# Two weight chunks ahead of x in the load queue and in the order of ScalarE and VectorE

## The chip, the cores and the metric

The kernel runs on one core of one Trainium2 chip. The metric is the device time of one execution in microseconds, as the median of several runs. Times inside the execution come from one profiled execution and count from the start of its span.

## The reference

One layer of a streaming encoder is computed in float32 for 512 prompt tokens and 32 sample tokens, T = 544 tokens of width 1024:

```python
r = x + 0.5 * rms_norm(swiglu_ffn(rms_norm(x, norm_ffn1_pre), w_ffn1_gate_up, w_ffn1_down), norm_ffn1_post)
z = rms_norm(r, norm_mix_pre) @ w_in          # then window attention and a gated short convolution
r = r + rms_norm(mixed @ w_out, norm_mix_post)
r = r + 0.5 * rms_norm(swiglu_ffn(rms_norm(r, norm_ffn2_pre), w_ffn2_gate_up, w_ffn2_down), norm_ffn2_post)
gate = sigmoid(rms_norm(r, norm_ple_pre) @ w_ple_gate)
r = r + rms_norm(gate * (p @ w_ple_proj), norm_ple_post)
```

The two feed-forward layers have an inner width of 2816, so the gate and up matrix is 1024 x 5632. Only the very beginning matters here: x, its norm, and the first columns of w_ffn1_gate_up.

## The kernel before

Features lie on partitions and tokens on the free axis. The 544 tokens are two halves A and B of 272. The residual r, and x_hi and x_lo made of it, have 8 feature tiles each (KD = 8).

Every float32 product is made of three matmuls in a rounded format: the weight is rounded to w_hi on ScalarE (`split_hi`, line 474), and the rest w_lo = raw - w_hi is made on VectorE (`split_lo`, line 796). The same holds for x: x_hi is r times a gain, rounded, on ScalarE (line 489), and x_lo is the rest, on VectorE (line 826). The products are w_hi x_hi, w_lo x_hi and w_hi x_lo.

Weights come in chunks of 128 columns, 512 KB each in the up stages (rows of 512 bytes), into four slots `raw`, `w_hi`, `w_lo`. The load of chunk c waits for w_lo of chunk c - 4. All large loads are issued by SyncE into one queue in program order: four tiles of x_prompt (512 KB each, rows of 4 KB), x_sample (128 KB), weight chunks 0 to 3, then some small gain rows and the copies of cache rows (`load_gains`), then the other weight chunks in loops.

Each engine has an order of its own, written out by hand; semaphores join them. At the start:

- TensorE turns x with transposes (line 1326): for each feature tile k four of 128 tokens into PSUM, then the sample's. The first four wait for the four x tiles one by one. Then comes the first pass of up1 on half A (`hi_pass`, line 1247): w_hi and w_lo times x_hi for chunks 0 and 1 over all k, then for chunks 2 and 3. Each chunk's first matmul waits for its w_lo (`up_ready`). In the pass of chunks 2 and 3, ahead of k = 2, stands the sum of the squares over partitions (`all_sums(0)`, line 1234). Then `lo_pass` (line 1255) adds w_hi times x_lo for the four chunks. Half B follows in the same form; its first matmul waits until VectorE has scaled half A's first gate result out of PSUM (line 834). From there on loops of full products (lines 1217 to 1219) run.
- VectorE copies the even feature tiles of r out of PSUM (line 943) and ScalarE the odd ones (line 597). VectorE squares half A's tiles (`first_square`, line 936) into two alternating buffers `sq`; GpSimd adds each to `ssq` (lines 418, 421). Square k waits for addition k - 2.
- ScalarE makes x_hi of half A in pairs, and rounds chunks 0 and 1 between them (`if k in (4, 6)`), then chunks 2 and 3. Then it goes on with half B: x_hi and squares, with the root of the first sum after the third tile.
- VectorE does square 4, w_lo 0, squares 5 and 6, w_lo 1, square 7, w_lo 2, x_lo of A tiles 0 to 3, w_lo 3, x_lo of A tiles 4 to 7, then the reciprocal of the root (line 802), x_lo of B, and the scaling of the first results.

Of the kernel before, what the change touches and what calls it, by code (L numbers as in the profile page):

```python
# [17 lines left out]
def encoder_layer(nc, t):  # L18
# [16 lines left out]
    KD = D // P  # L35
# [22 lines left out]
    chunks = units = 0  # L58
    for name, n, un, kt in STAGES:
        C0[name], U0[name] = chunks, units  # L60
        chunks, units = chunks + n, units + un
# [7 lines left out]
    def loaded_value(c):  # L69

        return 16 * sum(loads_of[c % SLOTS:c + 1:SLOTS])
# [33 lines left out]
    with ctx:  # L105
# [164 lines left out]
        def half(tile, k, h):  # L270
            return tile[:, k, h * HT:(h + 1) * HT]
# [36 lines left out]

        @block.sync
        def _(sp):  # L310
            def load_up(s, i):
                for j in range(4):
                    c = C0[s] + j
                    if isinstance(i, int):
                        if c + 4 * i >= SLOTS:
                            sp.wait_ge(lo_made, c + 4 * i - SLOTS + 1)
                    else:
                        sp.wait_ge(lo_made, i * 4 + (c - SLOTS + 1))
                    sp.dma_start(raw[:, c % SLOTS, 0:KD, :], up[s][j % 2, i * 2 + j // 2])\
                        .then_inc(w_loaded[c % SLOTS], 16)  # L320

            def load_down(s, i):
                for j in range(4):
                    c = C0[s] + j
                    sp.wait_ge(lo_made, i * 4 + (c - SLOTS + 1))
                    sp.dma_start(raw[:, c % SLOTS], down[s][i * 2 + j // 2, j % 2])\
                        .then_inc(w_loaded[c % SLOTS], 16)

            def load_short(cs):
                for c in cs:  # L330
                    sp.wait_ge(lo_made, c - SLOTS + 1)
                    for dst, src in chunk_loads(c):
                        sp.dma_start(dst, src).then_inc(w_loaded[c % SLOTS], 16)

            def load_gains():
                rows = "a (k p) -> (a k) p"
                for name in ("norm_ffn1_post", "norm_mix_pre", "norm_mix_post", "norm_ffn2_pre", "norm_ffn2_post",
                             "norm_ple_pre", "norm_ple_post"):
                    sp.dma_start(g_rows[COL[name]:COL[name] + KD, :], t[name].rearrange(rows, p=P)).then_inc(g_in, 16)
                for name, n, src in (("norm_conv_out", KA, t["norm_conv_out"].rearrange(rows, p=P)),  # L340
                                     ("conv_w", 3 * KA, t["conv_w"].rearrange("a j (k p) -> (a j k) p", p=P)),
                                     ("cache_conv", 2 * KA, t["cache_conv"].rearrange("a b j (k p) -> (a b j k) p", p=P))):
                    sp.dma_start(g_rows[COL[name]:COL[name] + n, :], src).then_inc(g_in, 16)
                at = COL["norm_attn_out"]
                for e in range(2):
                    sp.dma_start(g_rows[at:at + KA, e * DH:(e + 1) * DH],
                                 t["norm_attn_out"][0, e * DA // 2:(e + 1) * DA // 2].rearrange("(k p) -> k p", p=DH))\
                        .then_inc(g_in, 16)

                for name in "kv":  # L350
                    sp.dma_start(t[f"new_{name}_sample"][0, 0, 0:WINDOW - DEC], t[f"cache_attn_{name}"][0, 0, DEC:WINDOW])\
                        .then_inc(state_moved, 16)

            for i in range(XT - 1):
                sp.dma_start(x_tok[:, i, :], t["x_prompt"][0, i * P:(i + 1) * P, :]).then_inc(x_in[i], 16)
            sp.dma_start(x_tok[0:DEC, XT - 1, :], t["x_sample"][0]).then_inc(x_in[XT - 1], 16)
            for s, d in (("up1", "down1"), ("up2", "down2")):
                load_up(s, 0)
                if s == "up1":
                    load_gains()  # L360
                with sp.Fori(1, UP_GROUPS) as i:
                    load_up(s, i)
                with sp.Fori(0, DOWN_GROUPS) as i:
                    load_down(d, i)
                if s == "up1":
                    mix, flat, rows = C0["mix"], "a b w g d -> (a b w) (g d)", "a b j (k p) -> (a b j k) p"
                    load_short(range(mix, mix + SLOTS))

                    sp.wait_ge(unit_done, U0["mix"])
                    for name, dst in (("k", k_cache), ("v", v_cache)):  # L370
                        sp.dma_start(dst[:], t[f"cache_attn_{name}"][0, 0].rearrange("w g d -> w (g d)")).then_inc(cache_in, 16)
                    sp.dma_start(sinks[:], t["attn_sinks"].to_broadcast([P, 8])).then_inc(sink_in, 16)
                    load_short(range(mix + SLOTS, mix + 4 * SLOTS))
                    sp.wait_ge(band_ready, 3)
                    for name, prompt, sample in (("k", k_new[:], k_own[:]), ("v", v_band[:, NCH - 2, :], v_own[:])):
                        sp.dma_start(t[f"new_{name}_prompt"].rearrange(flat), prompt).then_inc(state_stored, 16)
                        sp.dma_start(t[f"new_{name}_sample"].rearrange(flat)[WINDOW - DEC:WINDOW, :], sample)\
                            .then_inc(state_stored, 16)
                    load_short(range(mix + 4 * SLOTS, C0["up2"]))
                    sp.wait_ge(conv_out, 1)  # L380
                    for name, at in (("prompt", 0), ("sample", 2 * KA)):
                        sp.dma_start(t[f"new_conv_{name}"].rearrange(rows, p=P), conv_new[at:at + 2 * KA, :])\
                            .then_inc(state_stored, 16)
# [82 lines left out]
        def _(act):  # L466
            def split_hi(c, i=0):

                n, s = width_of[c], c % SLOTS
                act.wait_ge(w_loaded[s], i * 16 + loaded_value(c))  # L470
                if c >= SLOTS:
                    semaphore, value, per = used(c - SLOTS)
                    act.wait_ge(semaphore, i * per + value)
                nc.scalar.activation(w_hi[:, s, 0:n, :], raw[:, s, 0:n, :], ACT.Copy).then_inc(hi_made, 1)  # L474
# [115 lines left out]
            act.dma_start(g_rows[0:KD, :], t["norm_ffn1_pre"].rearrange("a (k p) -> (a k) p", p=P)).then_inc(g_first_in, 16)  # L590
            act.wait_ge(consts, 4)
            nc.scalar.activation(rms_first[:], eps[:], ACT.Sqrt)
            act.wait_ge(g_made, 1)
            for k in range(KD):
                if k % 2:
                    act.wait_ge(x_turned, k + 1)
                    nc.scalar.activation(r[:, k, 0:SEQ], misc[:, k % 4, :], ACT.Copy).then_inc(r_loaded_act, 1)
                    act.wait_ge(r_loaded, k // 2 + 1)
                    high(0, k - 1, A)
                    act.wait_ge(r_loaded_act, k // 2 + 1)  # L600
                    high(0, k, A)
                if k in (4, 6):
                    split_hi(k // 2 - 2)
            split_hi(2), split_hi(3)
            act.wait_ge(r_loaded, KD // 2 + 1)
            up_stage("up1", 0, KD, 1)
# [184 lines left out]
        def _(dve):  # L791
            def split_lo(c, i=0):

                n, s = width_of[c], c % SLOTS
                dve.wait_ge(hi_made, i * 4 + (c + 1))
                nc.vector.tensor_tensor(w_lo[:, s, 0:n, :], raw[:, s, 0:n, :], w_hi[:, s, 0:n, :].bitcast(F32),  # L796
                                        ALU.subtract).then_inc(lo_made, 1)
# [133 lines left out]
            def first_square(k):  # L931

                if k >= 2:
                    dve.wait_ge(summed, k - 1)
                dve.wait_ge(r_loaded_act if k % 2 else r_loaded, k // 2 + 1)
                nc.vector.tensor_tensor(sq[:, k % 2, :], half(r, k, A), half(r, k, A), ALU.mult)\
                    .then_inc(first_squared, 1)

            dve.wait_ge(turned_g, 1)
            nc.vector.tensor_copy(gT[:, 0:KD], bank[:, 0, 0:KD]).then_inc(g_made, 1)  # L940
            for k in range(0, KD, 2):
                dve.wait_ge(x_turned, k + 1)
                nc.vector.tensor_copy(r[:, k, 0:SEQ], misc[:, k % 4, :]).then_inc(r_loaded, 1)
                first_square(k // 2)
            dve.wait_ge(x_turned, KD + 1)
            nc.vector.tensor_copy(r[:, :, SEQ:T], bank[:, 3, 0:KD * DEC].rearrange("p (k n) -> p k n", k=KD))\
                .then_inc(r_loaded, 1)
            first_square(4)
            split_lo(0)
            first_square(5), first_square(6)  # L950
            split_lo(1)
            first_square(7)
            split_lo(2)
            chain_lo(0, A, range(0, 4))
            split_lo(3)
# [149 lines left out]
            for v in range(2, len(MIX_UNITS)):  # L1105
# [12 lines left out]
                if v == 32:  # L1118
                    for s, at in enumerate((SEQ, T + 2)):
                        i = nc.vector.tensor_copy(conv_rows[:, s], cinp[:, :, at:at + 2].rearrange("p k r -> p r k"))  # L1120
# [487 lines left out]
```

## Time and profile before

| | |
|---|---|
| median of 3 runs | 1155.08 us (1153.62 to 1156.03) |
| span of the profiled execution | 1152.4 us |
| TensorE busy | 1107.6 us (96%) |
| VectorE busy | 570.2 us (49%) |
| ScalarE busy | 422.3 us (37%) |
| GpSimd busy | 133.5 us (12%) |
| moved by DMA | 94.28 MB, mean 82 GB/s |

The span goes from the first to the last instruction on the engines; what lies around it in a timed run is not part of it. The busy shares are means over the whole span. The change touches its first 40 us, so the stretches of that part must be read by themselves.

### The profile page before, as it was taken

To read this page: it belongs to the slowest core of one execution; us is meant where nothing else is said; L and a number is where in the kernel's file an instruction comes from. 1 tells how busy PE (TensorE), PEld (TensorE's weight loads), DVE (VectorE), ACT (ScalarE), POOL (GpSimd) and SP (SyncE) were. 2 spreads that over 40 slices of the span, in tenths; PEclk is the share of its full clock that TensorE was granted. 3 is DMA by queue.
4 is the path that set the end of the run, shared out by engine and by line. 5 is a ranking of instruction groups with operands and counts; after the bars stand their busy time and mean duration, and the time that the engine had idled before them with its cause. 6 is when DMAs were issued, how large, how long until landed. Compare 5 with 4: busy or idle time off the path is not lost.

```text
span 1152.4 us, 21208 instructions
## 1 busy us (share of the span) xinstructions
PE 1107.6 (96%) x8503; PEld 1076.5 (93%) x8503; DVE 570.2 (49%) x1029; ACT 422.3 (37%) x803; POOL 133.5 (12%) x154
## 2 busy tenths in 40 slices
PE   5999999999999999999989889999999999998896
PEld 5999999999999999877888889999999999998896
DVE  6644445444312268556593784445444421226743
ACT  4533333223222254423444562333323322225563
POOL 3100000000011132000213420000000001113211
PEclk8999999999999999999999999999999999999899
DMA  7232333223333205121032222233322333333002
GB/s 212 73 91 73 89 93 105 77 73 102 99 101 100 74 20 121 32 60 55 20 110 74 74 67 80 73 91 94 106 73 73 110 95 98 101 92 88 24 1 78
DMA packets 182644, 94.28 MB, mean 82 GB/s; under 512 B 11768, under 2 KB 180928, under 8 KB 182592
## 3 DMA queue, kind: packets, MB, share of 16 engines
q1 hardware_dynamic: 182576, 93.56, 28.4%
q8 instruction: 36, 0.59, 0.2%
q14 instruction: 16, 0.13, 0.0%
q10 hardware_dynamic: 16, 0.00, 0.0%
HBM read 91.15 MB, written 2.50 MB: 81 GB/s over the span
## 4 chain that ended last, share of the span: by engine, by line
PE 85%; DVE 10%; ACT 2%; POOL 1%; issue 1%; DMA 1%; SPq 0%; DVEq 0%; POOLq 0%; ACTq 0%
PE bank L1219 25%; PE bank L1217 25%; PE bank L1218 25%; PE bank L1247 3%; DVE x_lo L826 2%; PE misc L1326 2%; PE misc L1389 2%; DVE w_lo L796 2%; PE misc L1368 1%; POOL ssq L421 1%; DVE r L817 1%; ACT w_hi L474 1%; PE bank L1255 1%; DVE rpre L802 1%; DVE misc L802 1%
## 5 line engine op out<-in xcount | busy, mean ns | idle before, releaser
L1217 PE MATMUL bank<-x_hi,w_hi 128*128 128x272 f32 x1600 | 464.9, 291 | 5.2 <-DVE tG L1154 3.3
L1219 PE MATMUL bank<-x_hi,w_lo 128*128 128x272 f32 x1600 | 464.6, 290 | 0.0
L1218 PE MATMUL bank<-x_lo,w_hi 128*128 128x272 f32 x1600 | 461.2, 288 | 0.0
L796 DVE TENSOR_TENSOR w_lo<-raw,w_hi 128x1024 fp32r<-128x1024 f32 (+2 forms) x154 | 206.6, 1348 | 275.9 <-ACT w_hi L474 275.9
L1217 PEld LDWEIGHTS bank<-x_hi,w_hi 128*128 128x128 f32 x1600 | 302.3, 189 | 9.6 <-issue 6.7
L1218 PEld LDWEIGHTS bank<-x_lo,w_hi 128*128 128x128 f32 x1600 | 302.9, 189 | 0.1
L1219 PEld LDWEIGHTS bank<-x_hi,w_lo 128*128 128x128 f32 x1600 | 302.0, 189 | 0.0
L474 ACT ACTIVATE w_hi<-raw 128x1024 fp32r<-128x1024 f32 (+2 forms) x154 | 173.7, 1135 | 177.4 <-PE bank L1219 161.6
L1219 PE MATMUL bank<-h_hi,w_lo 128*128 128x272 f32 x704 | 204.5, 290 | 0.0
L1217 PE MATMUL bank<-h_hi,w_hi 128*128 128x272 f32 x704 | 204.2, 290 | 0.0
L1218 PE MATMUL bank<-h_lo,w_hi 128*128 128x272 f32 x704 | 203.0, 288 | 0.0
L421 POOL TENSOR_TENSOR ssq<-ssq,sq 128x272 f32<-128x272 f32 x112 | 108.0, 964 | 253.0 <-ACT sq L479 242.2
L1218 PEld LDWEIGHTS bank<-h_lo,w_hi 128*128 128x128 f32 x704 | 133.3, 189 | 0.2
L1217 PEld LDWEIGHTS bank<-h_hi,w_hi 128*128 128x128 f32 x704 | 133.0, 189 | 0.2
L1219 PEld LDWEIGHTS bank<-h_hi,w_lo 128*128 128x128 f32 x704 | 133.0, 189 | 0.0
L505 ACT ACTIVATE tG<-tG 128x272 f32<-128x272 f32 x88 | 38.0, 431 | 132.7 <-DVE tG L834 132.7
L418 POOL COPY ssq<-sq 128x272 f32<-128x272 f32 x16 | 10.9, 683 | 620.2 <-ACT sq L479 611.3
L511 ACT ACTIVATE h_hi<-tU 128x272 f32 (+1 forms) x88 | 38.0, 431 | 122.0 <-DVE tU L843 122.0
L1247 PE MATMUL bank<-x_hi,w_hi 128*128 128x272 f32 x224 | 64.3, 317 | 11.1 <-DVE w_lo L796 3.8
L836 DVE TENSOR_TENSOR tU<-bank,rpre 128x272 f32<-128x272 f32 x88 | 38.4, 436 | 66.7 <-PE bank L1219 66.7
L845 DVE TENSOR_TENSOR h_lo<-tU,h_hi 128x272 f32 (+1 forms) x88 | 39.3, 447 | 62.2 <-ACT h_hi L511 62.2
L479 ACT ACTIVATE sq<-bank 128x272 f32<-128x272 f32 x48 | 18.9, 393 | 118.8 <-PE bank L1219 116.1
(160 smaller groups left out, 1073.0 us busy)
## 6 DMA issues: line engine op xcount, KB each, us to landing
raw<-w_ffn_gate_up SPq DMA_DIRECT2D x88, 512.0 KB, 3.9
raw<-w_ffn_down SPq DMA_DIRECT2D x32, 704.0 KB, 4.7
raw<-w_in SPq DMA_DIRECT2D x14, 512.0 KB, 3.9
raw<-w_ple_gate SPq DMA_DIRECT2D x8, 512.0 KB, 3.9
x_tok<-x_prompt SPq DMA_DIRECT2D x4, 512.0 KB, 5.0
raw<-w_in SPq DMA_DIRECT2D x8, 256.0 KB, 4.2
raw<-w_out SPq DMA_DIRECT2D x16, 128.0 KB, 2.9
raw<-w_out SPq DMA_DIRECT2D x8, 256.0 KB, 3.4
```

What stands on the lines that cost most here:

```text
L421: nc.gpsimd.tensor_tensor(dst, dst, sq[:, s % 2, :], ALU.add).then_inc(summed, 1)
L474: nc.scalar.activation(w_hi[:, s, 0:n, :], raw[:, s, 0:n, :], ACT.Copy).then_inc(hi_made, 1)
L505: nc.scalar.activation(tG[:, j, :], tG[:, j, :], ACT.Silu).then_inc(gate_act, 1)
L511: nc.scalar.activation(half(h_hi, i * 2 + j, h), tU[:, j, :], ACT.Copy).then_inc(h_hi_made, 1)
L796: nc.vector.tensor_tensor(w_lo[:, s, 0:n, :], raw[:, s, 0:n, :], w_hi[:, s, 0:n, :].bitcast(F32), ALU.subtract).then_inc(lo_made, 1)
L802: nc.vector.reciprocal(dst, sum_bank(n)).then_inc(inverted, 1)
L836: nc.vector.tensor_tensor(tU[:, j, :], psum(u + 1), rpre[:, h, :], ALU.mult).then_inc(u_scaled, 1)
L845: nc.vector.tensor_tensor(half(h_lo, i * 2 + j, h), tU[:, j, :], half(h_hi, i * 2 + j, h).bitcast(F32), ALU.subtract).then_inc(h_ready[h], 1)
L1217: nc.tensor.matmul(psum(u), wh, hi, start=(k == 0), stop=False)
L1218: nc.tensor.matmul(psum(u), wh, lo, start=False, stop=False)
L1219: mm = nc.tensor.matmul(psum(u), wl, hi, start=False, stop=(k == n - 1))
L1247: nc.tensor.matmul(psum(u), w[:, c % SLOTS, k, :], half(x_hi, k, h), start=(k == 0 and w is w_hi), stop=False)
```

## The change

The loads of chunks 0 and 1 are issued ahead of x, those of chunks 2 and 3 stay behind it. ScalarE rounds chunks 0 and 1 ahead of its first work on x (before it waits for the first gains), and VectorE makes their w_lo right behind its copy of the first gains, ahead of its first copy of x. Squares 4 to 7 then stand together.

```diff
-            def load_up(s, i):
-                for j in range(4):
+            def load_up(s, i, chunks=range(4)):
+                for j in chunks:
...
+            load_up("up1", 0, range(2))
             for i in range(XT - 1):
                 sp.dma_start(x_tok[:, i, :], t["x_prompt"][0, i * P:(i + 1) * P, :]).then_inc(x_in[i], 16)
...
-                load_up(s, 0)
+                load_up(s, 0, range(2 if s == "up1" else 0, 4))
...
             nc.scalar.activation(rms_first[:], eps[:], ACT.Sqrt)
+            split_hi(0), split_hi(1)
             act.wait_ge(g_made, 1)
...
-                if k in (4, 6):
-                    split_hi(k // 2 - 2)
             split_hi(2), split_hi(3)
...
             nc.vector.tensor_copy(gT[:, 0:KD], bank[:, 0, 0:KD]).then_inc(g_made, 1)
+            split_lo(0), split_lo(1)
             for k in range(0, KD, 2):
...
-            first_square(4)
-            split_lo(0)
-            first_square(5), first_square(6)
-            split_lo(1)
-            first_square(7)
+            for k in range(KD // 2, KD):
+                first_square(k)
             split_lo(2)
```

## Rows read from the trace of the kernel before

**Rows 1.** The page: span, busiest engine, and the chain by engine.
```profile
span 1152.4 us, 21208 instructions
...
PE 1107.6 (96%) x8503; PEld 1076.5 (93%) x8503; DVE 570.2 (49%) x1029; ACT 422.3 (37%) x803; POOL 133.5 (12%) x154
...
PE 85%; DVE 10%; ACT 2%; POOL 1%; issue 1%; DMA 1%; SPq 0%; DVEq 0%; POOLq 0%; ACTq 0%
```

**Rows 2.** Stretches: length, busy per engine, granted clock, DMA share, GB/s.
```profile
3.00:8.00 5.00, 1.67 (x4) 0.73 (x4) 0.17 (x1) 0.00 (x0) 0.00 (x0) 1.00 1.00 388
9.00:15.00 6.00, 6.00 (x32) 5.83 (x31) 3.77 (x7) 4.54 (x9) 1.94 (x3) 1.00 1.19 288
15.40:17.80 2.40, 0.10 (x2) 0.00 (x0) 2.34 (x5) 2.40 (x6) 1.86 (x2) 1.00 0.20 46
17.90:20.70 2.80, 0.75 (x2) 0.43 (x2) 2.80 (x4) 2.21 (x3) 2.28 (x3) 0.50 0.57 162
20.80:24.50 3.70, 3.70 (x16) 3.70 (x17) 3.70 (x5) 1.91 (x5) 3.18 (x4) 0.50 0.63 174
24.60:26.60 2.00, 2.00 (x17) 1.95 (x16) 2.00 (x3) 0.00 (x1) 1.09 (x2) 0.99 0.81 237
...
35.80:37.00 1.20, 0.00 (x0) 0.00 (x0) 1.20 (x4) 0.04 (x1) 0.00 (x0) 1.00 0.00 0
...
50.00:1145.00 1095.00, 1070.53 (x8261) 1041.80 (x8261) 534.17 (x976) 396.67 (x757) 118.03 (x130) 0.99 0.28 79
```

**Rows 3.** The chain that ended last, in its first 80 us: start, us, what.
```profile
26.13 1.15 DVE w_lo L796
...
31.23 5.35 DVE x_lo L826 x8
...
37.08 6.27 PE bank L1247 x48
```

**Rows 4.** Timeline of TensorE: start, us, operation, idle before it and releaser.
```profile
8.81 6.08 PE L1326 MATMUL misc<-ident,x_tok 128*128 128x128 f32 x29 [1.19 <-DMA x_tok<-x_prompt]
...
17.86 0.57 PE L1247 MATMUL bank<-x_hi,w_hi 128*128 128x272 f32 x1 [2.35 <-ACT x_hi L489]
...
20.78 0.59 PE L1247 MATMUL bank<-x_hi,w_hi 128*128 128x272 f32 x1 [2.13 <-DVE w_lo L796]
...
27.32 0.39 PE L1247 MATMUL bank<-x_hi,w_hi 128*128 128x272 f32 x1 [0.55 <-DVE w_lo L796]
...
28.18 0.62 PE L1234 MATMUL misc<-ssq,ones 128*128 128x272 f32 x2
```

**Rows 5.** Timeline of VectorE around the squares of x.
```profile
16.54 1.21 DVE L796 TENSOR_TENSOR w_lo<-raw,w_hi 128x1024 fp32r<-128x1024 f32 x1
...
18.60 0.43 DVE L936 TENSOR_TENSOR sq<-r 128x272 f32<-128x272 f32 x1
18.95 1.78 DVE L796 TENSOR_TENSOR w_lo<-raw,w_hi 128x1024 fp32r<-128x1024 f32 x1
20.65 0.99 DVE L936 TENSOR_TENSOR sq<-r 128x272 f32<-128x272 f32 x1
21.57 1.21 DVE L796 TENSOR_TENSOR w_lo<-raw,w_hi 128x1024 fp32r<-128x1024 f32 x1
```

**Rows 6.** Timeline of GpSimd: additions of the squares.
```profile
13.85 0.77 POOL L421 TENSOR_TENSOR ssq<-ssq,sq 128x272 f32<-128x272 f32 x1 [0.94 <-DVE sq L936]
...
21.72 1.69 POOL L421 TENSOR_TENSOR ssq<-ssq,sq 128x272 f32<-128x272 f32 x1 [0.38 <-DVE sq L936]
```

**Rows 7.** SyncE's queue: four chunks issued; the page's line with us to landing.
```profile
3.48 7.56 SPq L319 DMA_DIRECT2D raw<-w_ffn_gate_up  x4
...
raw<-w_ffn_gate_up SPq DMA_DIRECT2D x88, 512.0 KB, 3.9
```

**Rows 8.** Timeline of ScalarE: rounding of chunks 2 and 3.
```profile
17.70 2.00 ACT L474 ACTIVATE w_hi<-raw 128x1024 fp32r<-128x1024 f32 x2
```

**Rows 9.** Transposes by tile: ns min/median/max, first and last start.
```profile
L1326 PE MATMUL misc<-ident,x_tok x32: 272/421/477, 4.6 to 14.6; 128*128 128x128 f32 x32
...
L1326 PE MATMUL misc<-ident,y_gain x32: 270/273/327, 1128.6 to 1144.6; 128*128 128x128 f32 x32
```

## The prediction

> **What bounds the kernel now.** I read the page first. TensorE is busy 96% of a 1152.4 us span and carries 85% of the chain that ended last; VectorE has 10% of it [rows 1]. Between 50 and 1145 us TensorE is busy 1070.5 of 1095 us [rows 2]. Nothing of the change touches that stretch: after the first four weight chunks every load, rounding and split stands in the same order behind the same waits. What the change can move is the moment from which TensorE runs through, and whatever moves that moment moves the end by the same amount.
>
> So I read the chain in order of time through the head of the kernel. It goes from x to the last of the four w_lo (26.13 to 27.3), to the first sum over squares on TensorE (28.18), and through the root on ScalarE and the reciprocal on VectorE to eight x_lo on VectorE (31.23 to 36.58). Then come the first scaled gate and the eight-chain of token half B on TensorE at 37.08 [rows 3, 4]. TensorE stands still from 35.8 to 37.0 [rows 2], so VectorE sets 37.08. I look at its timeline, since its order of work is what the change rewrites.
>
> VectorE has nothing to do until x comes: the last x tile is first turned at 8.81 [rows 4], and from 15.4 to 17.8 it is busy 2.34 of 2.40 us, from 17.9 to 24.5 all of it [rows 2]. Two of its operations there, the w_lo of chunks 0 and 1, start at 16.54 and 18.95 [rows 5] and do not depend on x. The change takes them out of this stretch and pays with a later x. The question is which of the two is larger.
>
> **Part 1, the load queue: x comes later.** The queue moves in order, so all of x moves behind two chunks of 524,288 bytes. In 9 to 15 us, when the queue holds only weight chunks, it moves 288 GB/s; in 3 to 8 us, when it holds x, it moves 388 GB/s [rows 2]. The two chunks take 2 x 0.524 MB / 288 GB/s = 3.64 us. The start of the queue on an empty chip with weights in front is not shown, so I bound it: if weights went at x's rate it would be 2 x 0.524 / 388 = 2.70 us; if the change from one kind to the other costs some 0.3 us on top, 3.9. I take 3.6, the rate of the very same transfers, so the last x tile is turned first at 12.4 instead of 8.81. The issue of the loads costs nothing beyond that: the four chunks took 7.56 us to issue [rows 7] only because the queue was full, and with two chunks and x in it x is at least as near to moving as the queue's head. Chunks 2 and 3 land when they did, since the bytes ahead of them are the same, and by 15.4 the queue is all but empty (46 GB/s) [rows 2]; their first use moves from 17.7 [rows 8] to about 20. The gains behind them are not needed for tens of us.
>
> The Trainium skill, DMA: Bandwidth & Descriptors, section Specifications, puts the smallest transfer that runs at line rate at 512 B. By that rule the weights' 512-byte rows would cost no more than x's 4 KB rows, and the delay would be 2.7 instead of 3.6 us. The measured 288 against 388 GB/s speaks against it.
>
> **Part 2, ScalarE: two roundings leave.** The roundings of chunks 0 and 1 ran between the copies of x and x_hi. They now run at about 4.7 and 6.6 us (a chunk lands 3.9 us after its issue [rows 7], here at 0.7, and the second 1.8 later), where ScalarE waits for x anyway. Here and below I use the clock of before and add the 3.6 at the end. x_hi 6 and 7 end at 16.5 instead of 17.7, and chunk 2's and 3's roundings (2.00 us from 17.70 [rows 8]) end at 18.5. The four w_lo of chunk 2 and 3 need them only later, so by itself this brings nothing on the path.
>
> **Part 3, VectorE: two splits leave.** w_lo 0 runs from 16.54 to the next start at 17.68 (1.14 us) and w_lo 1 from 18.95 to 20.65 (1.70 us) [rows 5]: 2.84 us less behind x. They now run at about 6 to 9 us, in cover: VectorE waits for the first copy of x, then at about 13 us, so 4 us of slack stand behind them. But all 2.84 is not won. The squares of x alternate with GpSimd's additions: square k waits for addition k-2, and the two buffers are shared. In before the w_lo filled those waits. An addition takes 0.77 alone, and 1.69 when it starts beside a w_lo (21.72), ending 0.63 after that w_lo [rows 5, 6]; a square starts 0.35 before the next operation (18.60, 18.95) [rows 5]. Without filler, from 16.54, which is where square 4 ends: square 5 0.36, addition 4 0.63, its semaphore 0.15, addition 5 ahead of square 6 0.63, squares 6 and 7 0.72, addition 6 ahead of w_lo 2 0.63. Together 3.12, so w_lo 2 starts at 19.7 instead of 21.57: the gain is 1.9 us. Its bounds are 1.6 (each addition 0.77) and 2.84 (no stall). From there to w_lo 3 the order is unchanged.
>
> Sum so far: w_lo 3 comes 3.6 - 1.9 = 1.7 us later, and so does all that hangs on it.
>
> **Part 4, TensorE: a new pause ahead of the critical sum.** In before the first pass of chunks 0 and 1 starts at 17.86, stops for w_lo 1 until 20.78 and hands over to chunks 2 and 3 at about 26.6, so that only 0.55 us are lost before 27.32 [rows 3, 4]. After the change the pass follows the turning of x directly. In before's clock it runs from 15.4 to about 19.4 (32 matmuls at 0.12), and then TensorE waits: two matmuls when w_lo 2 is there (20.8), the rest when w_lo 3 is (25.3). Two gaps of 1.4 and 4.3 us stand where one of 0.55 was. In before, the granted clock is 0.50 (1.2 GHz) from 17.9 to 24.5, behind a pause of 2.4 us with 0.10 us of work in it, and back at 1.00 (2.4 GHz) after 3.7 us of work [rows 2]. There the slow stretch cost nothing, because TensorE was ahead of w_lo 3. Now it would lie behind it. At half clock 16 matmuls took 3.70 us, at full clock 17 took 2.00 [rows 2], that is 0.23 against 0.12 each. Six of them and the sum over squares, which showed 0.62 at full clock, stand between w_lo 3 and the root: 6 x 0.11 = 0.6, plus 0.3 to 0.5 for the sum. I take 0.9 us. TensorE's own path then: 64 matmuls at 0.12 and the sum's 0.6 from 29.0 on, 16 of the matmuls slow: 29.0 + 8.3 + 1.8 = 39.1. That is just ahead of VectorE's 37.08 + 1.7 + 0.9 = 39.7, so VectorE still decides.
>
> The sum is +1.7 + 0.9 = +2.6 us. The profiled execution has a span of 1152.4, and the median of the runs is 1155.1, 2.7 us more, which I take as what lies around the span. Only the difference is carried over: 1155.1 + 2.6 = 1157.7.
>
> **The rivals.**
> - *The clock stays up, or is up sooner.* If the two matmuls at w_lo 2 or the place of the pause keep the clock at 1.00, part 4 is nothing: +1.7, 1156.8. The turning of x may gain too: the median transpose there took 421 ns where the last ones of the kernel take 273 [rows 9], though the clock is printed as 1.00, so for most of them the engine was slow; if it quickens sooner after the later x, up to 1 us comes back, 1155.8. For it: the head of the trace shows one fall only, and there is work on both sides of the new pause. Against it: that one fall came after 2.4 us, and the pause here has 4.3.
> - *Stalls smaller and loads quicker.* Weights at 2.7 us, gain 2.84: -0.1, and with the clock +0.8: 1155.0 to 1155.9. For it: the two bounds. Against it: each is the far end.
> - *Faster.* The loads overlap so well that x is not later than by about 1 us; then the gain of 1.9 wins, and with the clock or without it is -0.9 to -2.8, 1152.3 to 1154.2. It decides the sign from the point at which x's delay is below the gain. Against it: both rates are steady for microseconds, and DMA is busy all through 3 to 15 us.
> - *The clock stays down longer.* If 26 of the 64 matmuls are slow, TensorE's own path ends at 29.0 + 8.3 + 2.9 = 40.2, and with the sum later too +3.5: 1158.6.
>
> **How the numbers follow.** Forecast 0.45 (own range 1157.1 to 1158.4), clock up 0.25, stalls smaller 0.13, faster 0.08, clock down longer 0.09. 0.2% is 2.3 us, about what a measurement of this kernel can tell from no change. The forecast lies just outside it, at +2.6; 0.04 of its 0.45 falls inside. So faster 0.08, same 0.25 + 0.13 + 0.04 = 0.42, slower 0.50. The range leaves out the faster case and the lower half of the smaller stalls (0.14) and a tail above (0.05): 1155.4 to 1159.0.
>
> **What would show it.** The first turning of the last x tile at 12.4 (part 1). w_lo 0 and 1 over by 9 us (part 3). Squares 5 to 7 with idle VectorE between them, and w_lo 2 starting at about 23.3. The first pass of chunks 0 and 1 from about 19 without a stop, then a pause and w_lo 3 ending near 29. The granted clock at 0.50 in the slices behind that. Half B's first matmul at 39.7, and all later stages as before. The prediction is wrong if x is late by less than 2.7 us or more than 3.9, if VectorE is not the last before half B, or if the later stages differ.

## The result

| | before | changed |
|---|---|---|
| median, seven runs each | 1153.64 us (1152.91 to 1156.03) | 1157.26 us (1156.19 to 1159.14) |
| span of the profiled execution | 1152.4 us | 1155.5 us |
| ratio to before | | 1.0024, 95% interval 1.0013 to 1.0035 |

The change makes the kernel slower, by 0.24%, which is 2.8 us, and the whole interval lies above 1 (1.5 to 4.0 us). The two medians alone lie 3.6 us apart, inside that interval. Beside the experiments the kernel before had medians of 1154.83 to 1155.04 over 23 to 29 runs, so 1153.64 is a low one. The forecast was +2.6 us.

Nothing large shows on the page of the changed kernel. Line numbers have moved by up to two (1247 is 1245, 1217 is 1215).

```profile
span 1155.5 us, 21208 instructions
...
PE 1107.5 (96%) x8503; PEld 1075.6 (93%) x8503; DVE 569.5 (49%) x1029; ACT 422.6 (37%) x803; POOL 132.0 (11%) x154
...
PE 83%; DVE 10%; ACT 3%; POOL 2%; issue 1%; DMA 1%; SPq 0%; DVEq 0%; POOLq 0%; ACTq 0%
```

Busy times are those of before to within 1.5 us per engine, as they must be: the same instructions run. The chain carries two per cent less TensorE and one more each of ScalarE and GpSimd. Two per cent are about 20 us, and TensorE's whole part of the chain in the first 40 us of before is under 8, so the chain also takes other ways through the later joints between stages, and its shares say little on the change.

The stretches of the changed kernel answer to [rows 2]; the columns are length, busy per engine, granted clock, DMA share and GB/s.

```profile
3.00:7.00 4.00, 0.00 (x0) 0.00 (x0) 1.10 (x1) 1.47 (x2) 0.00 (x0) 1.00 1.12 328
7.00:11.00 4.00, 0.95 (x2) 0.36 (x2) 1.35 (x2) 0.64 (x1) 0.00 (x0) 1.00 1.02 410
...
24.50:28.50 4.00, 0.16 (x2) 0.00 (x0) 4.00 (x6) 1.16 (x3) 2.31 (x4) 0.70 0.46 131
26.60:28.50 1.90, 0.00 (x0) 0.00 (x0) 1.90 (x3) 0.00 (x0) 0.50 (x1) 0.50 0.43 130
28.60:32.80 4.20, 4.20 (x16) 3.97 (x17) 2.63 (x5) 1.54 (x5) 0.24 (x1) 0.50 0.47 128
33.00:35.00 2.00, 2.00 (x18) 2.00 (x17) 1.97 (x3) 2.00 (x6) 1.71 (x3) 1.00 0.00 0
```

The first two rows show the new order of the queue: weights at 328 GB/s (by 7 us some 1.5 MB have moved and the two chunks are 1.05, so the end of this stretch is x already; the single stretches 3 to 4 and 4 to 5 us have 329 and 328), then x at 410. From 24.5 to 28.5 TensorE has almost nothing to do, which is the new pause. The granted clock falls to 0.50 in it, near 26.1, and stays there through the first 4.2 us of work behind it.

The timeline of TensorE, which answers to [rows 4], shows the same as single operations.

```profile
12.99 4.77 PE L1324 MATMUL misc<-ident,x_tok 128*128 128x128 f32 x29 [1.44 <-DMA x_tok<-x_prompt]
...
18.30 0.39 PE L1245 MATMUL bank<-x_hi,w_hi 128*128 128x272 f32 x1
...
24.15 0.39 PE L1245 MATMUL bank<-x_hi,w_hi 128*128 128x272 f32 x1 [1.55 <-DVE w_lo L796]
...
28.59 0.59 PE L1245 MATMUL bank<-x_hi,w_hi 128*128 128x272 f32 x1 [3.93 <-DVE w_lo L796]
...
39.50 0.36 PE L1245 MATMUL bank<-x_hi,w_hi 128*128 128x272 f32 x1 [0.43 <-DVE tG L834]
```

The last x tile is turned 4.18 us later than before, and the turning of the other tiles is quicker (4.77 against 6.08 us). The first pass follows without a wait, and then come the two pauses for w_lo 2 and w_lo 3. Half B starts at 39.50 instead of 37.08.

So the way from x to half B can be cut into four pieces. The start of the sample tile's transposes marks the end of the turning.

| piece | before | changed | difference |
|---|---|---|---|
| first turning of the last x tile, at | 8.81 | 12.99 | +4.18 |
| from there to the end of the turning | 6.01 | 4.70 | -1.31 |
| to the end of w_lo 3 | 12.44 | 10.85 | -1.59 |
| to the root on ScalarE | 1.58 | 2.72 | +1.14 |
| to half B's first matmul | 8.24 | 8.24 | 0.00 |
| half B starts at | 37.08 | 39.50 | +2.42 |

The spans differ by 3.1 us. The 0.7 us that half B does not carry come from later stages, which are looked at under the prediction.

### The profile page after: what moved, and what is told of

The parts are those of the page before. It is cut to its first block, busy times and chain, and to the rows that moved or that the text cites. A ratio compares the mean times of both kernels' runs of the same rounds, so it can differ in the third digit from the quotient of the medians.

```text
span 1155.5 us, 21208 instructions
## 1 busy us (share of the span) xinstructions
PE 1107.5 (96%) x8503; PEld 1075.6 (93%) x8503; DVE 569.5 (49%) x1029; ACT 422.6 (37%) x803; POOL 132.0 (11%) x154
## 4 chain that ended last, share of the span: by engine, by line
PE 83%; DVE 10%; ACT 3%; POOL 2%; issue 1%; DMA 1%; SPq 0%; DVEq 0%; POOLq 0%; ACTq 0%
PE bank L1217 25%; PE bank L1215 25%; PE bank L1216 25%; DVE x_lo L826 2%; PE bank L1245 2%; PE misc L1324 2%; PE misc L1387 2%; DVE w_lo L796 2%; POOL ssq L422 1%; PE misc L1366 1%; DVE r L817 1%; DVE rpre L802 1%; DMA x_tok<-x_prompt 1%; DVE misc L802 1%; ACT w_hi L475 1%
```

## The experiments

Each experiment was timed in five rounds beside the kernel before on the same chip. The ratios carry intervals of 0.09% to 0.17% on each side, which is 1 to 2 us, so they can tell only the larger differences. The smaller ones are read from the traces, where half B's start follows a chain of single operations. There is one trace of each kernel, and the head scatters too: in the four kernels with both chunks ahead of x in the queue and x turned by the same operations, the last x tile came between 12.93 and 13.39 and the turning took 4.70 to 5.45 us. "Half B" is its first matmul, and "turning" is the time from the first transpose of the last x tile to the first one of the sample tile.

| kernel | last x tile | turning | w_lo 3 ends | to the root | half B | ratio to before |
|---|---|---|---|---|---|---|
| before | 8.81 | 6.01 | 27.26 | 1.58 | 37.08 | 1 |
| changed | 12.99 | 4.70 | 28.54 | 2.72 | 39.50 | 1.0024 (1.0013 to 1.0035) |
| loads alone | 13.22 | 5.13 | 31.11 | 1.72 | 41.05 | 1.0043 (1.0026 to 1.0060) |
| order of engines alone | 8.69 | 10.74 | 30.02 | 1.57 | 39.93 | 1.0037 (1.0022 to 1.0053) |
| changed, pauses filled | 13.39 | 5.09 | 29.36 | 1.56 | 39.16 | 1.0015 (1.0002 to 1.0027) |
| changed, w_lo 2 earlier | 12.93 | 5.45 | 28.84 | 2.73 | 39.80 | 1.0023 (1.0013 to 1.0034) |
| before, warm | 8.61 | 4.96 | 26.32 | 1.67 | 36.22 | 0.9993 (0.9980 to 1.0005) |
| one chunk ahead | 11.15 | 5.77 | 28.44 | 1.58 | 38.24 | 0.9998 (0.9987 to 1.0010) |
| changed, three repairs | 12.80 | 3.41 | 27.37 | 1.57 | 37.17 | 1.0000 (0.9990 to 1.0011) |
| before, warmer | 10.02 | 3.35 | 26.51 | 1.73 | 36.48 | 0.9998 (0.9989 to 1.0006) |
| before, warmer and filled | 9.58 | 3.35 | 26.12 | 1.58 | 35.94 | 1.0001 (0.9991 to 1.0011) |

### The loads alone

```diff
+            load_up("up1", 0, range(2))
             for i in range(XT - 1):
...
-                load_up(s, 0)
+                load_up(s, 0, range(2 if s == "up1" else 0, 4))
```

> The kernel before with the load order of the change alone: weight chunks 0 and 1 ahead of x, roundings and w_lo where they were. My theory (x late against work taken off VectorE): the last x tile is turned first at 13.0 us, as in the changed kernel. Behind it VectorE has the two w_lo again, so w_lo 3 ends at 30.1 to 30.7 us instead of 28.5, and half B starts at 40.3 us, or 41.4 if the clock is at half behind w_lo 3; the time is 1.0 to 2 us above the changed kernel, ratio to before 1.003 to 1.004. Rival (moving the roundings and w_lo is worth nothing, only the load order counts): half B at 39.5 as in the changed kernel, ratio 1.0024.

The last x tile came at 13.22, w_lo 3 ended at 31.11 and half B started at 41.05, for a ratio of 1.0043. That is 1.6 us later than the changed kernel at half B, and 2.57 us later at w_lo 3. VectorE has the two w_lo between its squares again:

```profile
20.38 1.21 DVE L797 TENSOR_TENSOR w_lo<-raw,w_hi 128x1024 fp32r<-128x1024 f32 x1
21.52 1.35 DVE L937 TENSOR_TENSOR sq<-r 128x272 f32<-128x272 f32 x2
22.80 1.78 DVE L797 TENSOR_TENSOR w_lo<-raw,w_hi 128x1024 fp32r<-128x1024 f32 x1
```

The rival, that moving the work is worth nothing, falls by the trace: from the end of the turning to the end of w_lo 3 it is 12.76 us, and 10.85 with the work moved. The intervals of the two times overlap. The late x alone is dear, and the moved work gives part of it back. It does not pay a slow clock behind w_lo 3 (1.72 us to the root), so the net gain of the moved work at half B is smaller than its gain at w_lo 3. The expectation of 40.3 was 0.7 us too early, because x came 0.2 us later, and the turning (0.43 us more than in the changed kernel) and the way to w_lo 3 were longer than assumed.

### The order of the engines alone

```diff
-            load_up("up1", 0, range(2))
...
-                load_up(s, 0, range(2 if s == "up1" else 0, 4))
+                load_up(s, 0)
```

> The changed kernel with the loads as they were: x first, then four chunks, but ScalarE and VectorE still take chunks 0 and 1 ahead of x. My theory: both engines stand in front of x until chunk 1 has landed (near 12.8 us), VectorE's first copy of x comes at about 15.1 instead of 9.3 us, w_lo 3 ends near 29.3, half B starts at 39.2, or 40.3 with the clock at half: ratio to before 1.002 to 1.003, so the new order of the engines needs the new order of the loads. Rival (the order of the engines costs nothing, the late x is all): ratio 1.000, half B at 37.1.

VectorE's first copy of x came at 15.08, as expected, behind w_lo 1. TensorE shows who was held up:

```profile
8.69 3.04 PE L1323 MATMUL misc<-ident,x_tok 128*128 128x128 f32 x13 [1.12 <-DMA x_tok<-x_prompt]
15.82 3.68 PE L1323 MATMUL misc<-ident,x_tok 128*128 128x128 f32 x16 [4.10 <-DVE r L943]
```

The first 16 transposes fill the four PSUM banks; the rest stand for 4.10 us until VectorE has emptied one. Half B started at 39.93, 0.7 us later than expected, ratio 1.0037. There was a pause of 3.24 us ahead of w_lo 3 here too, but the granted clock fell only at about 31.5, behind the sum over squares (30.93), so the root came 1.57 us behind w_lo 3. TensorE was then at half clock until about 34.9, went through to half B without a pause, and was its last path by some 0.1 us (8.34 from the root instead of 8.24). Neither half of the change stands alone, and the two together are less bad than either (1.0024), though the intervals overlap.

### The pauses filled

```diff
+FILL1, FILL2 = 12, 30
...
                 if units[2:4]:
+                    if ci == 0 and h == A:
+                        pe.wait_ge(r_loaded_act, KD // 2)
+                        fill(FILL1)
+                        (u2, c2, ready2), (u3, c3, ready3) = units[2:4]
+                        ready2()
+                        fill(FILL2)
                     hi_pass(units[2:4], x_hi, h, lambda k: None, second)
...
+            def fill(n):
+                for _ in range(n):
+                    nc.tensor.matmul(misc[:, 3, 0:HT], w_hi[:, 0, 0, :], half(x_hi, 0, A), start=True, stop=True)
```

> The changed kernel with matmuls that nobody needs (42 of 272 columns into a free PSUM bank) in TensorE's two pauses ahead of w_lo 2 and w_lo 3. If the clock at half behind the pause costs what I say, the granted clock stays at 1.00, the time from the end of w_lo 3 to the root falls from 2.7 to 1.6 us, and half B starts at 38.4 instead of 39.5: 1.1 us less than the changed kernel, ratio to before 1.0015. Rival (the clock is beside the path, or does not depend on the pause): half B at 39.5, ratio 1.0024 or more.

The granted clock stayed at 1.00 through the former pause. The first fence is the stretches of this kernel, the second its chain behind w_lo 3, and the third the chain of the changed kernel:

```profile
22.50:28.50 6.00, 5.95 (x48) 5.73 (x47) 5.77 (x7) 2.31 (x6) 4.85 (x6) 1.00 0.37 100
28.60:30.90 2.30, 2.14 (x16) 1.84 (x15) 2.30 (x5) 0.00 (x0) 0.00 (x0) 1.00 0.04 11
```

```profile
29.42 1.01 PE bank L1246 x6
30.43 0.47 PE misc L1233 x2
```

```profile
28.59 1.73 PE bank L1245 x6
30.32 0.92 PE misc L1232 x2
```

Six matmuls take 1.01 instead of 1.73 us, and the sum 0.47 instead of 0.92. From the end of w_lo 3 to the root it is 1.56 instead of 2.72. That 1.16 us is the price of the clock, and the empty pauses are its cause: nothing but work in the two pauses was added. Half B came only 0.34 us sooner, not 1.1, because in this execution x was 0.40 us later and the turning 0.39 us longer. The ratio of 1.0015 is the expected one, but its interval overlaps that of the changed kernel, so the gain is shown by the trace and not by the time.

### w_lo 2 between the squares

```diff
-            for k in range(KD // 2, KD):
-                first_square(k)
-            split_lo(2)
+            first_square(4), first_square(5), first_square(6)
+            split_lo(2)
+            first_square(7)
```

> The changed kernel with w_lo 2 between squares 6 and 7 instead of behind square 7. If VectorE's two idle pieces of 0.67 us between the squares are GpSimd's additions, one of them goes: w_lo 3 ends 0.4 to 0.7 us sooner (27.9 instead of 28.5), and half B starts near 38.9; ratio 0.0005 below the changed kernel. Rival (the additions of GpSimd then come later and the same time is lost at x_lo): no change.

In the changed kernel VectorE stands still twice between the squares, each time until an addition of GpSimd is over:

```profile
18.92 1.25 DVE L936 TENSOR_TENSOR sq<-r 128x272 f32<-128x272 f32 x2
20.84 0.44 DVE L936 TENSOR_TENSOR sq<-r 128x272 f32<-128x272 f32 x1 [0.67 <-POOL ssq L422]
21.95 0.44 DVE L936 TENSOR_TENSOR sq<-r 128x272 f32<-128x272 f32 x1 [0.67 <-POOL ssq L422]
22.31 1.78 DVE L796 TENSOR_TENSOR w_lo<-raw,w_hi 128x1024 fp32r<-128x1024 f32 x1
```

With w_lo 2 ahead of square 7 one of the two pieces went, and the end of w_lo 3 came 10.46 us behind the end of the turning instead of 10.85. That 0.39 is the lower end of what was expected. More had been won on the way: w_lo 3 started 8.69 us behind the end of the turning instead of 9.64. But it then took 1.77 instead of 1.21 us, as w_lo 2 does behind an addition of GpSimd, so 0.56 of the 0.95 us was lost again. That is in part the rival, that the additions come later and cost the same time elsewhere.

```profile
21.62 1.80 DVE L796 TENSOR_TENSOR w_lo<-raw,w_hi 128x1024 fp32r<-128x1024 f32 x1
27.07 1.77 DVE L796 TENSOR_TENSOR w_lo<-raw,w_hi 128x1024 fp32r<-128x1024 f32 x1
```

At half B nothing of it is seen, because the turning was 0.75 us longer in this execution. The clock stayed at half to about 34.4, so TensorE's own path came level with VectorE's. Its x_lo pass started at 35.73, and half B followed with no idle time before it:

```profile
35.73 4.11 PE L1253 MATMUL bank<-x_lo,w_hi 128*128 128x272 f32 x32
39.80 0.36 PE L1245 MATMUL bank<-x_hi,w_hi 128*128 128x272 f32 x1
```

It cost nothing all the same: from the root to half B it is 8.23 us, as in the changed kernel. The condition of the prediction's fourth rival, the clock down longer, was met, and its price was not paid. The ratio did not change.

### Before, with TensorE kept busy while x comes

```diff
+WARM, WARM_X = 10, 4
...
+            for _ in range(WARM):
+                turn(bank[:, 1, 0:P], ident[:])
             pe.wait_ge(g_first_in, 16)
...
                     if k == 0:
+                        if i:
+                            for _ in range(WARM_X):
+                                turn(bank[:, 1, 0:P], ident[:])
                         pe.wait_ge(x_in[i], 16)
```

> The kernel before with transposes that nobody needs ahead of and between the first tiles of x (10 from 1.7 us on, 4 behind each of the first tiles), into a free PSUM bank. If TensorE turns x at 1.2 GHz although the profile prints 1.00, the 29 transposes behind the last x tile fall from 6.0 us to 3.1 to 4, w_lo 3 ends 0.8 to 1.2 us sooner, half B starts at 36.0 to 36.3 instead of 37.1: ratio to before 0.999 to 0.9993. Rival (the turning is bound by the copies out of PSUM, or the clock was up): no change, 1.000.

The turning took 4.96 instead of 6.01 us, w_lo 3 ended 0.94 us sooner and half B started 0.86 us sooner, at 36.22; 0.20 of it is an earlier x. So about 1 us of the six was the clock, although the profile of before prints 1.00 through all of them. The turning did not come down to 4 us; the median transpose still took 391 ns. The trace shows why: the few transposes between the tiles did not keep the clock up. In this kernel the profile does record a fall, just as the last tile comes, and a rise near 12.1:

```profile
8.00:12.00 4.00, 3.39 (x16) 3.39 (x17) 2.17 (x4) 1.74 (x4) 0.46 (x2) 0.58 1.19 268
12.00:14.00 2.00, 2.00 (x22) 1.83 (x20) 1.63 (x4) 2.00 (x5) 1.23 (x2) 0.99 1.20 290
```

These rows have the columns of [rows 2]. The ratio of 0.9993 fits, with 1 inside its interval.

### One chunk ahead

```diff
-            load_up("up1", 0, range(2))
+            load_up("up1", 0, range(1))
...
-            split_hi(0), split_hi(1)
+            split_hi(0)
...
                     high(0, k, A)
+                if k == 4:
+                    split_hi(1)
...
-            split_lo(0), split_lo(1)
+            split_lo(0)
...
-            for k in range(KD // 2, KD):
-                first_square(k)
+            first_square(4), first_square(5), first_square(6)
+            split_lo(1)
+            first_square(7)
```

> Half of the change: chunk 0 alone ahead of x in the load queue, on ScalarE and on VectorE; chunk 1 is handled as before, with w_lo 1 between squares 6 and 7. The last x tile is turned first at 10.9 us (half the delay), w_lo 3 ends near 28.1, half B starts at 37.9, or 38.9 if the clock is at half behind w_lo 3: ratio to before 1.0007 to 1.0016, between the two kernels. Rival (a fixed cost of the new order, whatever the number of chunks): as the changed kernel, 1.0024.

The last x tile came at 11.15, 2.34 us after before and 1.84 ahead of the changed kernel. Half B started at 38.24, almost in the middle of the two. There is no fixed cost of the new order; each chunk ahead of x costs a share, but the two shares are made of different things. The first delayed x by 2.34 us and gained 0.92 between turning and w_lo 3, with no slow clock behind it. The second brought the slow clock (2.72 instead of 1.58 us to the root), and the quicker turning. The timed ratio of 0.9998 is below what was expected, and the upper end of its interval just takes in the 1.16 us of the trace.

### The changed kernel with three repairs

This is the filler of the pauses (6 and 32 matmuls), w_lo 2 between squares 6 and 7, and 36 useless transposes ahead of the first x tile and 5 ahead of each of the others.

> The changed kernel with three repairs at once: useless transposes ahead of x so that x is turned at full clock, useless matmuls in the two pauses so that the clock stays up, and w_lo 2 between squares 6 and 7. If the late x (4 us) is the only loss that is left and the three repairs give about 1, 1.1 and 0.4 us, half B starts at 37.0 to 37.5, as in the kernel before: ratio 1.000. Rival (the losses lie elsewhere): ratio above 1.0015.

x was as late as in the changed kernel, 12.80. The turning took 3.41 us, with a median transpose of 273 ns as at the end of the kernel [rows 9], and 1.57 us passed from w_lo 3 to the root:

```profile
L1336 PE MATMUL misc<-ident,x_tok x32: 272/273/329, 8.5 to 16.0; 128*128 128x128 f32 x32
```

Half B started at 37.17 and the ratio is 1.0000. The 4.0 us of late x are paid for by 2.60 us of quicker turning and 1.28 us less from its end to w_lo 3. The third repair cannot be seen by itself: that last way is 11.16 us long, more than the 10.85 of the changed kernel, and w_lo 3 took 1.79 us in it, as in the kernel with w_lo 2 earlier. So the account of the loss closes, in the trace and in the time.

### Warmer, and warmer and filled

Two attempts to better the kernel before: with 5, 8 and 12 useless transposes between the x tiles, and then also with transposes in the pauses ahead of w_lo 0, 1 and 3.

> The kernel before with more of the useless transposes between the first tiles of x (5, 8 and 12 instead of 4 each), so that the pauses of the turning are filled. Theory: the 29 transposes take 3.5 us (5.0 with fewer, 6.0 in before), w_lo 3 ends at 25.2 to 25.6, half B starts at 35.1 to 35.6: ratio to before 0.9983 to 0.9988. Rival (once VectorE's and ScalarE's copies bound the turning, no more is to be had): half B at 36.2 as with fewer.

> The same, with useless transposes also in the pauses ahead of w_lo 0, w_lo 1 and w_lo 3. Theory: the clock stays at 1.00 from the turning on, but in this order of loads the slow stretch lies ahead of w_lo 3 and costs nothing on the path, so half B starts within 0.4 us of the kernel without them: same ratio. Rival (the slow stretch now reaches past w_lo 3): up to 1.1 us less.

The transposes of the first ran at half clock for longer than I assumed and overran x: the last tile was turned first at 10.02 instead of 8.7. The turning took 3.35 us, about as expected (3.5), but half B started at 36.48, and not at 35.1 to 35.6; the rival had 36.2. The turning ended 0.20 us sooner than with fewer transposes, and w_lo 3 ended 0.19 us later, so a quicker turning was not passed on in full. What holds it up behind the turning was not tested.

Filling the pauses as well kept the granted clock at 1.00 throughout, and changed nothing behind w_lo 3 beyond 0.15 us (1.58 against 1.73 us to the root). That is the mechanism expected: with x first the slow stretch lies ahead of w_lo 3. Half B came 0.54 us sooner, outside the 0.4 that was stated, and 0.44 of it is that x was turned sooner. Half B is then 1.14 us ahead of before, but the time shows nothing of it (1.0001). Neither ratio differs from 1, so no kernel here is shown to be faster than the kernel before.

## Why the prediction was right, and where its terms were off

The sign and the size hold: +2.6 us forecast, +2.8 by the ratio, +2.4 at half B in the profiled execution. So do the three causes in the sum, late x, less work on VectorE and a slow clock behind the new pause. But two of the three signs of being wrong that the prediction names were met: x is late by more than 3.9 us, and the later stages differ. Only the third was not, since VectorE is the last before half B. The near hit is in part luck, as the terms show.

**Part 1, x later: 3.6 forecast, 4.18 measured.** This term was mis-sized, and beyond its upper bound of 3.9. The rate was not the reason: ahead of x the weights moved at 328 GB/s and not at 288 [rows 2], which alone gives 3.2. The step that failed is the sum itself, bytes divided by rate. The loads of one chunk and of two give the price that counts: the first x tile came at 4.58, 6.60 and 8.50 with none, one and two chunks ahead, so about 2.0 us per 512 KB. The last tile lost some 0.3 more, in both. In its first 3 us the queue had moved less than before (99 against 147 GB/s in 1 to 3 us), which is part of it. Where the rest lies, between the last byte and the landing, stays open. The rule of the Trainium skill (DMA: Bandwidth & Descriptors, section Specifications) that 512 B is enough for line rate would have given 2.7, an estimate with x's 388 GB/s; the runs speak against it, with 328 against 410 GB/s in one and the same kernel. No run varies the length of the rows alone.

**Parts 2 and 3, work taken from behind x: 1.9 forecast, 1.59 measured on VectorE.** w_lo 0 and 1 ran at 5.90 and 7.67, in cover. The squares stood still as described (0.67 us twice). From square 4's start to w_lo 2's it was 3.39 instead of 5.69 us, 2.3 less, and w_lo 2 then took 1.78 instead of 1.21, since addition 6 stood ahead of it. The sum of the two is 1.7. The forecast had an addition ahead of w_lo 2 and not the longer w_lo 2. Its lower bound is also mis-added: three additions at 0.77 give a gain of 1.5, not 1.6. The Trainium skill (SBUF — State Buffer, section "SBUF: two separate sides") says that such a pair of operations on VectorE and GpSimd holds a shared port in turn, each for its whole length. The traces agree: a w_lo that starts first keeps its 1.21 us, and the addition beside it takes 1.69 instead of 0.77 and ends 0.63 behind it; behind an addition it is w_lo that takes 1.78 [rows 5, 6]. What changed with the order was who waited for whom.

**The turning: up to 1 forecast as a rival, 1.31 measured.** I gave a quicker turning to the rivals, tied to a clock that stays up. It came together with the slow clock later. The row showed it beforehand, with a median of 421 against 273 ns [rows 9]. I read it rightly, but put it at a low chance beside the forecast and not into the sum. In the four kernels with both chunks ahead and no useless work between the tiles the turning took 4.70, 5.13, 5.09 and 5.45 us, so it belongs to the sum with a range. The moved roundings are not its cause, since the kernel with the loads alone has them back and 5.13 us. In before the transposes quicken about 5.7 us behind the first one of the last tile, in the changed kernel after 3.0, in the other three after 3.8 to 4.7, and with one chunk ahead after 5.1. What sets that point, and whether the late x itself moves it, stays open.

**Part 4, the new pause: 0.9 forecast, 1.14 measured.** It came at the place and by the mechanism described, and the kernel with filled pauses shows it as cause. The sum over squares cost 0.45 of the 0.3 to 0.5 forecast, where 0.9 in all takes the low end, and the matmuls 0.72 instead of 0.6. TensorE's own path ended at 39.07, just ahead of VectorE's, as forecast at 39.1; in two experiments it came level with it or 0.1 us behind. The rival with the clock down longer is priced at +3.5, while its own path of 40.2 gives 3.1.

**The net.** Three errors, x by +0.6, turning by -1.3 and the rest by +0.5, left -0.2. That the forecast is so near at half B is their cancelling, and that is luck: without the turning, which had no place in the sum, it would have been 1.1 us too low. The 2.7 us around the span do not hold either; the profiled run of the changed kernel took 1157.26 us with a span of 1155.5, so 1.8. Only the difference was carried over, so this did not touch the forecast.

**The carry-over.** That everything behind half B stays as it was holds up to the first down stage and no further. The tiles y_down and y_out as ScalarE writes them, with first and last start in us, are given for before, for the changed kernel, and then for the loads alone:

```profile
L517 ACT ACTIVATE y_down<-bank x32: 388/392/433, 301.1 to 1065.1; 128x272 f32<-128x272 f32 x16, 128x272 f32 x16
...
L517 ACT ACTIVATE y_out<-bank x16: 377/393/446, 609.1 to 653.3; 128x272 f32<-128x272 f32 x16
```

```profile
L518 ACT ACTIVATE y_down<-bank x32: 387/392/430, 303.4 to 1069.5; 128x272 f32<-128x272 f32 x16, 128x272 f32 x16
...
L518 ACT ACTIVATE y_out<-bank x16: 378/393/446, 611.9 to 657.7; 128x272 f32<-128x272 f32 x16
```

```profile
L518 ACT ACTIVATE y_down<-bank x32: 387/392/430, 305.0 to 1071.1; 128x272 f32<-128x272 f32 x16, 128x272 f32 x16
...
L518 ACT ACTIVATE y_out<-bank x16: 377/392/449, 613.6 to 659.2; 128x272 f32<-128x272 f32 x16
```

The first y_down is at 301.1 in before, 303.4 here and 305.0 with the loads alone, so it follows half B's 37.08, 39.50 and 41.05 to 0.1 us. The last y_out is 44.2 us behind the first in before and 45.8 here. Over all eleven kernels that piece has 44.2 to 46.8 us with no relation to the change. TensorE pauses in these joints too, and in the two traces that were looked at the granted clock falls in other pieces of them: it is 0.91 in 640 to 680 us in before, and 0.91 in 580 to 620 and in 660 to 680 in the changed kernel. That this is the cause of the scatter was not tested. From half B's start to the end of the span it is 1115.3 us in before and 1116.0 in the changed kernel, and 1112.2 (w_lo 2 earlier) to 1117.4 over all eleven. A single profile therefore carries some 5 us of scatter behind the place that was changed, which is more than any of the effects told here, and its span says nothing on them. The repeated timings and the traces of the head do.

## What to carry to other kernels

Work that is moved ahead of a load is free only if its own data do not have to come through the same queue: price the bytes put in front by the landing times of one load more and one less, against what the bottleneck engine really gains after the stalls that the moved work had filled. Then look at what TensorE does in the time that was won: finishing a stage sooner, only to wait longer for the next operand, can lower the clock, as here by 1.14 us, exactly ahead of the operation that the path needs. Where an effect is a thousandth of the time, read it at the first point behind the change that all later work hangs on, and not from the span. Even there one trace has its scatter, here 0.4 us in the landing of x and 0.75 in the turning.

## What the runs showed of the hardware

- The profile prints a granted clock of 1.00 for TensorE from the start, but the first transposes ran at half pace, 0.21 us apart. Their median is 421 ns in before and 273 ns in the kernel that had kept TensorE busy since 2.5 us, as at the end of the kernel. A clock printed ahead of the first change of it in a trace is not evidence; the durations are.
- After a pause the clock came back in these traces behind 3.8 us (before), 4.4 us (changed), 5.5 us (w_lo 2 earlier) and 6.0 us (loads alone) of full work. The same kernel with small changes can so lose 1.1 us at one place.
- The clock need not fall in the pause itself. In the kernel with the order alone it fell at about 31.5 us, 1.4 us after TensorE had gone back to work from a pause of 3.24 us.
- Weights in rows of 512 bytes moved at 288 to 328 GB/s, x in rows of 4 KB at 388 to 410, in the same queue.
